# Second layer's opening: value tiles on scaled, unnormed tokens first, the norm's root put on afterwards

## The reference

```python
def rms_norm(x, g):
    xf = x.astype(jnp.float32)
    y = xf * lax.rsqrt(jnp.mean(xf * xf, axis=-1, keepdims=True) + NORM_EPS)
    return (y * g.astype(jnp.float32)).astype(x.dtype)
...
        sh1, sc1, gt1, sh2, sc2, gt2 = jnp.split(mod[:, None, :], 6, axis=-1)
...
        h = modulate(rms_norm(x, norm1_g[l]), sh1, sc1)
        hc = modulate(rms_norm(xc, norm1_g[l]), csh1, csc1)
        qa, ka, va, qb, kb, vb, ga, gb = split_in_proj(h @ w_in[l])
...
        kb = rms_norm(kb, k_norm_g[l])
```

## Time and profile before

| what | value |
|---|---|
| time, median of 3 runs (lowest to highest) | 2369.88 us (2366.74 to 2370.13) |
| the profiled execution's own time | 2373.01 us |
| span of that execution in its profile | 2371.2 us |
| PE, DVE, ACT busy in the span | 97%, 69%, 50% |

### The profile page before, as it was taken

The page is one execution under the profiler, slowest core; times in us unless marked ns, Lnnn a source line. Parts: engine busy times, 40 slices in busy tenths (PEclk is TensorE's granted clock), DMA queues, the critical chain, the costliest instruction groups (busy, mean ns, idle before and its releaser), DMA issues.

```text
span 2371.2 us, 32918 instructions
## 1 busy us (share of the span) xinstructions
PE 2311.2 (97%) x12127; PEld 1975.8 (83%) x12127; DVE 1646.2 (69%) x2531; ACT 1189.1 (50%) x1911; POOL 222.4 (9%) x343
## 2 busy tenths in 40 slices
PE   8999999999999999999999999999999999999999
PEld 4888887888888998998878777898888887878787
DVE  5886676798688877777686787754333387379864
ACT  5647777733334431342647787343222365477641
POOL 0200000020001112211100000100000010011020
PEclk9999999999999999999999999999999999999999
DMA  7421111183334337447221111523222234522263
GB/s 293 160 70 47 48 48 47 45 304 133 116 125 142 107 112 240 133 145 259 99 93 54 54 45 58 196 83 104 98 97 99 90 120 151 185 79 77 88 206 115
DMA packets 72101, 282.41 MB, mean 119 GB/s; under 512 B 9120, under 2 KB 9184, under 8 KB 70032
## 3 DMA queue, kind: packets, MB, share of 16 engines
q1 hardware_dynamic: 43056, 162.94, 20.1%
q0 software_dynamic: 28896, 117.46, 14.2%
HBM read 245.76 MB, written 33.55 MB: 118 GB/s over the span
## 4 chain that ended last, share of the span: by engine, by line
PE 82%; DVE 7%; ACT 6%; issue 4%; DMA 1%; POOL 0%; ACTq 0%; DVEq 0%; SPq 0%; POOLq 0%
PE ps L217 23%; PE ps L218 22%; PE ps L219 22%; PE ps L1444 1%; PE ps L1445 1%; PE ps L1446 1%; PE ps L1378 1%; PE ps L1385 1%; DVE w_lo L213 1%; PE ps L845 1%; ACT w_hi L206 1%; PE ps L1427 1%; DVE inv L1608 1%; ACT pr L1507 1%; DVE maxes L1631 1%
## 5 line engine op out<-in xcount | busy, mean ns | idle before, releaser
L217 PE MATMUL ps<-h_hi,w_hi 128*128 128x512 f32 (+2 forms) x1592 | 575.6, 362 | 5.9 <-ACT th_g L1540 2.9
L218 PE MATMUL ps<-h_lo,w_hi 128*128 128x512 f32 (+2 forms) x1592 | 565.1, 355 | 0.0
L219 PE MATMUL ps<-h_hi,w_lo 128*128 128x512 f32 (+2 forms) x1592 | 564.4, 355 | 0.0
L213 DVE TENSOR_TENSOR w_lo<-w_raw,w_hi 128x1024 fp32r<-128x1024 f32 x256 | 319.2, 1248 | 181.4 <-ACT w_hi L206 181.0
L206 ACT ACTIVATE w_hi<-w_raw 128x1024 fp32r<-128x1024 f32 x256 | 269.3, 1053 | 233.4 <-PE ps L219 218.3
L217 PEld LDWEIGHTS ps<-h_hi,w_hi 128*128 128x128 f32 x1592 | 301.3, 189 | 56.5 <-issue 12.8
L219 PEld LDWEIGHTS ps<-h_hi,w_lo 128*128 128x128 f32 x1592 | 300.8, 189 | 44.1
L218 PEld LDWEIGHTS ps<-h_lo,w_hi 128*128 128x128 f32 x1592 | 301.6, 189 | 42.0 <-issue 2.4
L218 PE MATMUL ps<-q_lo,w_hi 128*128 128x512 f32 x720 | 256.3, 356 | 0.0
L217 PE MATMUL ps<-q_hi,w_hi 128*128 128x512 f32 x720 | 255.5, 355 | 0.0
L219 PE MATMUL ps<-q_hi,w_lo 128*128 128x512 f32 x720 | 254.5, 354 | 0.0
(11 more groups left out here) (461 smaller groups left out, 4262.3 us busy)
## 6 DMA issues: line engine op xcount, KB each, us to landing
w_raw<-in_stream SPq DMA_DIRECT2D x288, 512.0 KB, 3.3
wt_x<-in_ada_t POOLq DMA_DIRECT2D x24, 512.0 KB, 3.7
wt_h<-in_ada_t POOLq DMA_DIRECT2D x20, 512.0 KB, 5.2
wt<-in_ada_t POOLq DMA_DIRECT2D x16, 512.0 KB, 4.4
ada_raw<-in_ada SPq DMA_DIRECT2D x6, 1024.0 KB, 20.9
x_keep<-x POOLq DMA_DIRECT2D x8, 768.0 KB, 7.8
gates<-th_g POOLq DMA_DIRECT2D x16, 384.0 KB, 2.6
gates<-sg POOLq DMA_DIRECT2D x24, 256.0 KB, 2.3
```

The source lines that it names most:

```text
L213: nc.vector.tensor_tensor(w_lo[:, u % 3, :], raw[:, u % 2, :], w_hi[:, u % 3, :].bitcast(F32), ALU.subtract).then_inc(lo_ready, 1)
L217: nc.tensor.matmul(out_ap, lh, rh, start=start, stop=False)
L218: nc.tensor.matmul(out_ap, lh, rl, start=False, stop=False)
L219: return nc.tensor.matmul(out_ap, ll, rh, start=False, stop=stop)
```

## The change

- Layer 2's tiles now come as v0, v1, K0, K1, then the Q tiles; the weight stream is put in that order.
- While the first layer's last down-projection adds its chunks to x, ACT and DVE write scaled but unnormed tokens, x·s, high and low (`lead_high`, `lead_low`), and the shift as 2 more columns. PE multiplies v0 and v1 with these at once (`lead_unit`): 512 and 258 columns. The statistic stands within v0, the spread ahead of v1. The 32 `keep_awake` matmuls are gone.
- The two raw value tiles are copied out (`copy_raw`, ACT), multiplied with the root (`multiply_raw`, DVE) and shifted (`shift_raw`, ACT), within the loop that makes the normed chunks. K0 and K1 then take those chunks together, and the two transpositions stand within their products.
- For that, the modulation columns 74 to 79 are no more done in the down-projection but in layer 2's projection, one a step in the steps 4 to 9, with their own conditioning vector: a Silu on ACT in step 3, and behind it the table of Ln and Exp is loaded again. In the down-projection two columns a chunk are done in place of three.

```diff
+            def copy_raw(self, act, u, k, z):
+                act.wait_ge(unit_done, finished(u + k))
+                act_own.link(act, nc.scalar.activation(z, psf[:, 1024 * k:1024 * k + self.w], ACT.Copy))
+                nc.scalar.activation(small[:, 8 + 2 * k:10 + 2 * k], psf[:, 1024 * k + self.w:1024 * k + self.w + 2],
+                                     ACT.Copy).then_inc(self.copied_raw.sem, 1)
+            def multiply_raw(self, dve, k, z):
+                dve.wait_ge(self.copied_raw.sem, self.copied_raw.base + k + 1)
+                nc.vector.tensor_tensor(z, z, psf[:, 2048:2048 + self.w], ALU.mult).then_inc(self.rooted.sem, 1)
+            def shift_raw(self, act, k, z, done):
+                act.wait_ge(self.rooted.sem, self.rooted.base + k + 1)
...
                 else:
-                    e.wait_ge(lo_ready, base + 1)
-                    e.wait_ge(before_units.sem, before_units.base + 5)
-                    keep_awake(base, 12)
-                    norm.statistic(e)
-                    keep_awake(base, 6)
-                    norm.spread(e)
-                    keep_awake(base, 14)
-                    norm.first_units(e, base)
+                    e.wait_ge(before_units.sem, before_units.base + 6)
+                    norm.lead_unit(e, base, 0)
+                    norm.lead_unit(e, base, 1)
+                    norm.first_units(e, base + lead, lambda e, c, k: second(6 - c) if k and c in (5, 6) else None)
...
+                    if values_first and t == 2:
+                        copy(2)
+                        turn_or_norm(0)
+                        turn_or_norm(1)
+                        continue
...
+                    if values_first and t == 3:
+                        side.condition(e)
+                        nc.scalar.preload_act_table_set("natural_log_exp_and_others")
...
-                    if side and 2 <= t < T - 2:
+                    if side and 2 * (1 + values_first) <= t < T - 2:
                         side.column(e)
...
-            return [("K", 0, TOK, None, True, 1.0), ("v", 0, TOK, None, False, 1.0), ("K", 1, TOK, kg, True, 1.0),
-                    ("v", 1, TOK, None, False, 1.0)] + [("Q", j, w, qg if j >= 4 else None, True, sc) for j in Q_ORDER]
+            keys = [("K", 0, TOK, None, True, 1.0), ("K", 1, TOK, kg, True, 1.0)]
+            values = [("v", 0, TOK, None, False, 1.0), ("v", 1, TOK, None, False, 1.0)]
+            return ([keys[0], values[0], keys[1], values[1]] if layer == 0 else values + keys) + [("Q", j, w, qg if j >= 4 else None, True, sc) for j in Q_ORDER]
...
-                    side = Columns(60, 80, 5, [r_h["wt_h"][:, k, :] for k in range(4)], r_h["cb_h"], r_h["wt_out_h"][:, :],
-                                   {80: [(1, 0), (1, 1)]})
+                    side = Columns(60, 74, 5, [r_kv["wt"][:, k, :] for k in range(4)], r_kv["cb"], r_kv["wt_out"][:, :], {})
```

More of the change, by code:

```diff
@@ L532, in linear, with __init__ @@
                 return mm
-        def keep_awake(u, count):
-            for k in range(count):
-                nc.tensor.matmul(ps[:, 0, :], identR[:, :], w_hi[:, u % 3, 0:512], start=True, stop=True)
         class Norm:
             late = False
-            def __init__(self, groups, scale_of, shift_of, twice=False, out=(h_hi, h_lo), lead=0):
+            def __init__(self, groups, scale_of, shift_of, twice=False, out=(h_hi, h_lo), lead=0, rootless=False, shifts=None):
                 self.groups, self.scale_of, self.shift_of = groups, scale_of, shift_of
@@ L546, in __init__ @@
                 self.lead = lead
-                self.rootless = twice
-                if self.rootless:
-                    self.lead_used, self.lead_hi, self.lead_lo = signals("whole", times=CH - 1, high=CH, low=CH)
+                self.rootless, self.shifts = rootless, shifts
+                if rootless:
+                    extra = int(shifts is not None)
+                    self.lead_used, self.lead_hi, self.lead_lo = signals("whole", times=CH - 1, high=CH + extra, low=CH + extra)
+                    self.first_chunk = extra
+                    self.moving = [(0, SEQ, 0), (SEQ, CTX + 2, SEQ)] if extra else [(0, SEQ, SEQ)]
+                    self.statistic_at, self.spread_at = (5, 0) if extra else (CH - 1, 4)
+                    if extra:
+                        self.copied_raw, = signals("hidden", scaled=2)
+                        self.rooted, = signals("norm", rooted=2)
                 self.squared, self.summed, self.stat, self.rough, self.refined, self.spread_done, self.scaled, self.full, self.high, self.low = signals(
@@ L605, in lead_unit @@
                         mm.then_inc(self.lead_used.sem, 1)
+            def copy_raw(self, act, u, k, z):
[8 more added lines that the diff above has]
+                act.wait_ge(self.rooted.sem, self.rooted.base + k + 1)
+                for v, (s0, n) in enumerate(self.groups):
+                    ins = nc.scalar.activation(z[:, s0:s0 + n], z[:, s0:s0 + n], ACT.Identity, bias=small[:, 8 + 2 * k + v:9 + 2 * k + v])
+                    if v == 0:
+                        act_own.link(act, ins)
+                ins.then_inc(done.sem, 1)
             def wait_used(self, act, u, c):
@@ L742, in first_units @@
                             mm.then_inc(unit_done, 1)
-                        if between and c == 0 and k == 0:
-                            between(pe)
+                        if between:
+                            between(pe, c, k)
         def newton(e, sums, y, width, done=None, scaled=False):
@@ L931, in dve, with open_pe @@
                 split_lo(e, 1)
+            def open_pe(e, c, k):
+                if c == 0 and k == 0:
+                    columns_of(e, last)
             def open_act(e, c):
@@ L984, in project @@
             groups_of = lambda t: [LAT, CON] if width[t] == TOK else [LAT]
-            assert not normed[0] and kinds[0][0] != "v"
+            values_first = kinds[0][0] == "v"
+            assert not normed[0] and values_first == (stacked and lead > 0)
             def pe(e):
@@ L1109, in act @@
                     norm.root(e)
+                    if lead and not skip:
+                        norm.copy_raw(e, base, 0, zt[:, 0, :])
                     if lead:
@@ L1113, in act, with lead_act @@
                     e.wait_ge(counted, 2)
-                norm.shape(e, (lambda c: norm.open_act(e, c)) if opening else (lambda c: norm.wait_used(e, base, c)) if lead else None)
+                def lead_act(c):
+                    norm.wait_used(e, base, c)
+                    if not skip and c == 3:
+                        norm.copy_raw(e, base, 1, zt[:, 1, :])
+                    if not skip and c >= 6:
+                        norm.shift_raw(e, c - 6, zt[:, c - 6, :], copied)
+                norm.shape(e, (lambda c: norm.open_act(e, c)) if opening else lead_act)
                 if norm.passes == 2:
@@ L1137, in dve, with lead_dve @@
                     norm.refine(e)
-                    if lead:
+                    if skip:
                         split_lo(e, base + 3)
+                    else:
+                        e.wait_ge(column_done, column_count(74))
                     norm.scale_first(e)
-                norm.scale(e, (lambda c: norm.open_dve(e, c)) if opening else None)
+                    if not skip:
+                        split_lo(e, base + 3)
+                def lead_dve(c):
+                    if not skip and 4 <= c < 6:
+                        norm.multiply_raw(e, c - 4, zt[:, c - 4, :])
+                norm.scale(e, (lambda c: norm.open_dve(e, c)) if opening else lead_dve)
                 e.wait_ge(norm.low.sem, norm.low.base + CH)
@@ L1864, in dve @@
             def dve(e):
-                if following and not late and following.rootless:
+                if following and not late and following.shifts is None:
                     dve_own.link(e, nc.vector.tensor_tensor(gains, col("gf", 0, CH), col("ng2", 0, CH), ALU.mult))
```

91 lines of the change are left out of this document (55 added, 36 removed).

## The result

The changed kernel takes 2379.52 us (median of 6 runs, 2376.56 to 2385.15), the kernel before 2369.88: +9.6 us, a ratio of 1.0042 with a 95% interval of 1.0031 to 1.0053. The profiled execution is the slowest of the six (2385.15 us, span 2383.3). So I compare steps inside the profiles, counted from **T0**, where PE leaves the down-projection (the start of the first matmul behind its last product): 1129.94 before, 1127.31 after.

A forecast was written before the change was run, and what follows sets the result against it. Layer 2's projection was taken as bound by DVE, nearly full there: K1's norm at 1185.3 plus 57.0 us gives 1242.3 against 1232.54, so 2369.9 + 9.8 = 2379.7, forecast 2380 us, range 2372 to 2389.

The forecast's parts named there:

- The gain at PE: At the seam of the two layers: PE is through v0, v1, K0, K1 at 1168.4, 11.2 us ahead.
- The chain on ACT: Layer 2's projection: Silu, tables, K0's copies and lowering start K1's norm on DVE at 1185.3, 9.3 us later.
- DVE's sum: From K1's norm to the projection's end: DVE's work of 55.9 us plus a wait of 1.1, 57.0 us.
- Carried over whole: At the attention's start: DVE's delay of 9.8 us goes in full into the kernel's time.
- rival 2: Projection: PE's waits bring the half clock, three losses of 1.7 us, 5.1 in all, 2385 us; chance 0.15.
- Rival 3: At the seam: x·s comes so late that PE waits through v0; +21 us, 2391; chance 0.03.
- Rival 1: Projection: the gain comes through, 2367.8 or 2360.5 us; chance 0.09 faster, 0.11 about no change.

The follow-up runs named there:

- e1: The changed kernel with the Silu and its two table loads one step later on ACT, the six columns following by one step: 2377.40 us, ratio 1.0031.
- e2: The changed kernel with K0's lowering put behind K1's norm and turn in DVE's list: 2377.64 us, ratio 1.0035.
- e5: The kernel before with only columns 74 to 79 and their Silu moved into layer 2's projection, no lead, old tile order: 2378.57 us, ratio 1.0043.
- e9: The changed kernel with columns placed as in e7, K0's lowering and the value copies left where the change put them: 2371.68 us, ratio 1.0008.
- e6: The changed kernel with 24 matmuls on nothing ahead of PE's three waits at layer 2's attention start: 2378.03 us, ratio 1.0036.
- e4: The changed kernel with the edits of e2 and e3 together: 2367.51 us, ratio 0.9993.
- e7: As e4, but with 18 columns in the down-projection and the last two in DVE's pause while PE spreads the root: 2369.41 us, ratio 0.9998.
- e3: The changed kernel with columns 74 to 79 back in the down-projection, without Silu and table loads in the projection: 2373.00 us, ratio 1.0016.
- e8: As e7, with the four copies of the value tiles ahead of K0's copy in ACT's list: 2366.08 us, ratio 0.9986.
- e10: As e8, with 5, 1 and 7 matmuls on nothing ahead of three waits at the attention's start: 2365.36 us, ratio 0.9984.

## Why the prediction was right, point by point

**The gain at PE.** Forecast: 11.2 us ahead at the Q tiles. Measured: 38.17 behind T0 in place of 49.66, so 11.5.

**The chain on ACT.** Forecast for K1's norm: 9.3 us late; measured 8.7. Its parts: Silu and tables 4.5 (4.53), copies of K0 3.5 (3.47), lowering 1.9 (1.97). e1 takes the Silu from the chain and K1's norm moves by 3.83; e2 takes copies and lowering, and it moves by 5.25. Both were causes, and neither the only one.

The Trainium skill ("ScalarE: Activation LUTs", section "What ACT_TABLE_LOAD costs") adds a drain of 1380 ns to each load. Here the split stands 1.30 us behind the second load's start, and the Silu 1.29 behind the first: no drain is seen, and the measured rows decide.

**DVE's sum.** Forecast 57.0 with a pause of 1.1; measured 57.27 with 1.20. e5 and e9 split the loss: columns with their Silu alone +7.96 at the attention, lead alone +1.55, together 9.51, and the change has 9.49. So the two parts add up, and most of the loss comes from the columns' new place. They get there by different ways: in e5 the whole of it lies behind K1's norm, in the change 3.83 us lie ahead of it, on ACT, and 4.11 behind. And the split is not the only one, as e2 takes 4.26 us off without moving a column. One thing the sum did not say: of the columns' 7.3 us only 4.1 are lost on DVE, since without them the stretch from K1's norm to the attention is 53.16 in e9, not 50. There DVE waits for ACT again, 2.40 us for K1's copies and 1.20 and 0.79 for the norms of Q tiles:

```profile
1188.69 0.95 DVE L1238 TENSOR_TENSOR k_hi<-zt,k_hi 64x768 fp32r<-64x768 f32 x1 [2.40 <-ACT k_lo L1122]
```

The prediction has DVE waiting for PE in this stage before the change; the rows say that each of its pauses ends on ACT, the 3.46 us one on K1's copies (in the Q tiles ACT in turn waits for PE).

**Carried over whole.** Here the prediction was incomplete. It counted PE's lost clock as rival 2 and took the forecast without it. In the profile both hold: DVE's 9.49, and 2.2 us on top at the attention's start, with the half clock, which are gone in e6. In the median they cannot be seen apart (+9.6 is near the first alone); whether the half clock comes in some executions only is not shown. Where PE stood still within the Q tiles, the half clock behind it (0.91 over the stretch) was hidden: DVE has no pause there that PE ends.

That +9.6 and the forecast +9.8 lie 0.2 us apart is luck in part. T0 itself lies at 1126.65 (e4) to 1129.95 (e7) in the twelve profiles, 2.62 us apart in e3 and e4, which are alike up to there; and what follows the 13th maximum is from 2.69 us shorter (e9) to 3.04 us longer (the changed kernel) than before. What tests the mechanism is +9.49 at the attention against +9.8, with K1's norm and DVE's stretch each within 0.6 us of the forecast.

**The other rivals.** Rival 3 did not come: PE has no gap at T0. Rival 1, the gain coming through, needs K1's norm before 45.56 us behind T0 (1175.5 less 1129.94). Only e8 and e10 reach that, at 45.23 and 45.18, with columns and Silu out of the projection, K0's lowering behind and the value copies ahead; and they are the two that are faster. But that bound holds DVE's 57.0 us with the columns. Without them the bound lies later: e4, with its norm at 47.01, is at the attention 4.52 us earlier than before, nearly as early as e8 (4.66). The price of the lowering's place was undersized in the expectation of e2: 3.5 us, where e2 has 4.26 and e7 against e9 5.28.

What stays open: why e7's median is not below e4's, though its profile is 1.0 us ahead at the 13th maximum (behind that it loses 1.5 to e4's); and how often the half clock comes, since each kernel has one profile.

## What to carry to other kernels

Closing a gap on one engine is worth what the engine behind it can take up. Here PE's 11 us went to a stage in which DVE had 7 idle us in 56.5. Put in alone, new work did not shorten that idle time (e5), and with the late start it left DVE nearly without a pause, so that PE waited. Before moving work into such a stage, look at where in its lists the pauses stand and what the moved work is queued ahead of, its table loads and its users included; where lists are strict, an order of two pieces of work can decide whether closing the gap gains anything: with K0's lowering ahead of K1's norm the lead alone is at the attention 1.55 us later than before (e9), behind it 3.73 us earlier (e7).

## What the runs showed of the hardware that was not expected

The same waits of PE need not give the same clock. e4 and e7 have the same work on PE there and nearly the same first two waits at the attention's start. PE's waits in e4, then e7:

```profile
1229.85 0.44 PE L1497 MATMUL ps<-k_hi,qa 128*128 128x384 f32 x1 [1.22 <-DVE maxes L1701]
1231.57 0.39 PE L1497 MATMUL ps<-k_hi,qa 128*128 128x256 f32 x1 [0.30 <-DVE maxes L1701]
```

```profile
1233.93 0.45 PE L1499 MATMUL ps<-k_hi,qa 128*128 128x384 f32 x1 [1.23 <-DVE maxes L1703]
1235.66 0.39 PE L1499 MATMUL ps<-k_hi,qa 128*128 128x256 f32 x1 [0.29 <-DVE maxes L1703]
```

The stretches behind them, e4 and then e7:

```profile
1231.00:1237.00 6.00, 4.67 (x16) 3.33 (x15) 3.41 (x6) 0.59 (x1) 0.00 (x0) 0.57 0.17 62
```

```profile
1234.00:1240.00 6.00, 3.94 (x20) 2.84 (x20) 4.20 (x7) 0.59 (x1) 0.00 (x0) 1.00 0.39 127
```

0.57 in the one and 1.00 in the other; e4's clock falls behind the second wait, ahead of any third. e8 is another such case: its waits of 1.23, 0.30 and 1.75 us are those of e7 (1.23, 0.29 and 1.77), and of the kernel before (1.22, 0.30 and 1.75), which both keep 1.00. Behind the third, e8 has:

```profile
1236.00:1240.00 4.00, 4.00 (x14) 3.22 (x14) 0.00 (x0) 2.40 (x4) 0.00 (x0) 0.57 0.00 0
```

What went on further ahead differs (DVE is at the attention 98.1 us behind T0 in e4, 98.9 in e7), but no run here shows what decides. The Trainium skill ("TensorE: Matmul & The Clock Gate", section "HAM oscillation — how this bites in real kernels") says that waits of PE in a loop put it back to the half clock each time; e4 and e8 agree, and e7 does not show it. For a change of some us in 2370 this is noise to reckon with: behind the same waits one profile (e7) loses 0.06 us up to the 13th maximum, another (e8) 1.56.
